# Scatter by accumulation into the residual rows, without four planes, and the last pair of a loop written out

## The chip, the core and the metric

One core of a Trainium2 chip runs the whole program. The metric is the device time of one execution in microseconds. The kernel before took 1590.88 us (median of 3 runs, 1590.01 to 1591.29).

## The reference, cut to what matters

The program is one layer of a diffusion backbone: 512 latent tokens and 256 context tokens of 1024 channels go through a bidirectional gated recurrence (HGRN2) with its projections, and then through a mixture of experts. The change touches only the mixture of experts and the final norm:

```python
def moe(h, router_w, router_b, w1, b1, w2, b2):
    logits = (h @ router_w + router_b).astype(F32)
    top_v, top_i = lax.top_k(logits, TOP_K)          # 4 of 32 experts per token
    top_w = jax.nn.softmax(top_v, axis=-1)
    ...                                              # assignments sorted by expert, cut in blocks
    def block_ffn(args):
        tok, e = args
        z = h[tok] @ w1[e] + b1[e]                   # 1024 -> 2048
        z_glu, z_lin = jnp.split(z, 2, axis=-1)
        z_glu = jnp.minimum(z_glu, SWIGLU_LIMIT)
        z_lin = jnp.clip(z_lin, -SWIGLU_LIMIT, SWIGLU_LIMIT)
        act = z_glu * jax.nn.sigmoid(SWIGLU_ALPHA * z_glu) * (z_lin + 1.0)
        return act @ w2[e] + b2[e]                   # 1024 -> 1024
    ...
    return jnp.zeros_like(h).at[slot_tok].add(y)     # y: rows times their slot weight
```

The layer's output is rmsnorm(r + gate * moe(f)), where r is the residual after the mixer and f its modulated norm. Every token gets four expert outputs, each times its softmax weight, and they are summed. All is float32.

## The kernel before, in words

The first 500 us are the mixer; they are the same in both kernels. Then the routing tables are made, and the expert loop runs. A block is 32 tokens of one expert; a pair is two blocks (par 0 and par 1). Each block is one step. There are as many pairs as the routing needs (`n_pairs`, read by every engine from a small table), so the loop is a hardware loop; the first pair stands in front of it, written out. Weights of an expert are 12 MB (w1 8 MB in eight chunks, w2 4 MB in four) and come from DRAM into one of two places in SBUF (`arena` for par 0, `big_b` for par 1) when a step's expert is a new one. Because 32 tokens fill only a quarter of 128 partitions, every row of 1024 is held as four quarters of 256 in four groups of 32 partitions.

What each engine does in a step (i, par):

- SP (L475 to L503): for each of the eight w1 chunks and four w2 chunks it waits until TensorE has used the old one, and loads the next expert's, or raises the semaphore if the expert stays the same.
- POOL (L642 to L652): `gather` (L619) fetches the token rows of the step two ahead from `frows` in DRAM by an indirect DMA, indexed by `tok_n`; `scatter` (L625) writes the step's result rows `y_sb` to DRAM by an indirect DMA, indexed by `row_s`. Entries without a token have an index out of bounds and are left out.
- TensorE: `rest_of_z` (w1 chunks 6 and 7 of this step, and the bias), `next_z` (w1 chunks 0 to 5 of the next step), `slots_of` (a small product from which the indices of a later step come), and `second` (w2).
- ScalarE: the sigmoid. VectorE: `step` (L1437): the transpose of the next step's gathered rows (`transpose_x`), `moved_rows`, the index of a later step (`index`), the gating (`gated`), the one-hot tiles, and `weighted` (L1431), the step's result times its slot weight and the gate g2.

In the kernel before, the scatter goes to `yrows`, a DRAM tensor of 4 x 512 rows: a plane for each of the four choices k of a token. No two scatters write the same row. The index is token + 512 k; k is carried through the slot product as a further column (`kf`, `kw16[:, :, 0]`), and gives `row_n`. A scatter waits for its rows, and VectorE's `moved_rows` for the scatter of two steps before, because it uses the same index tile. Two empty scatters are issued ahead of the loop.

After the loop SP loads the residual rows `hrows` (512 KB in each of four tiles), b2 four times, and the two broadcast rows g2 and final_g. When both scatter semaphores have reached their count it loads the four planes, 8 MB, as eight pairs of planes (L513 to L517). TensorE puts the residual, the weighted b2 and the planes 2 and 3 into PSUM by products with the identity; VectorE adds planes 0 and 1 and the PSUM banks; ScalarE makes the sum of squares and the root; VectorE scales; SP stores (L518 to L520).

TensorE's loop (L1906) runs over all pairs but the first, and in its last step it also runs `next_z` and `slots_of` for a pair that doesn't exist; the weights' semaphores are raised for it without a load.

Of the kernel before, what the change touches and what calls it, by code (L numbers as in the profile page):

```python
# [5 lines left out]
F32 = mybir.dt.float32  # L6
BF16 = mybir.dt.bfloat16
# [7 lines left out]
P = 128  # L15
# [16 lines left out]
N_CONST = 16  # L32
# [31 lines left out]
def build(nc, x, c, ctx_in, c_ctx, mod_c, mod_w, mod_b, norm1_g, norm2_g, hg_w_in, hg_lb_logits, hg_norm_g,  # L64
          hg_w_out, router_w, router_b, moe_w1, moe_b1, moe_w2, moe_b2, final_g, out):
    frows = nc.dram_tensor("frows", [LAT, D], F32, kind="Internal").ap()
    yrows = nc.dram_tensor("yrows", [TOPK * LAT, D], F32, kind="Internal").ap()
# [3 lines left out]
    yquarters = yrows.rearrange("r (q n) -> (r q) n", q=QT)  # L71
    with ExitStack() as stack:
# [74 lines left out]
        msk16 = sb("msk16", [P, LT, E], BF16)  # L147
# [35 lines left out]
        oh, ohd = (late[:, n * 512:n * 512 + 512].rearrange("p (i k e) -> p i k e", i=LT, k=TOPK) for n in range(2))  # L183
# [27 lines left out]
        kf = sb("kf", [P, LT * TOPK])  # L211
# [3 lines left out]
        row_n = [sb(f"row_n{i}", [P, 1], U32) for i in range(2)]  # L215
# [53 lines left out]
        ygat = arena[:, 0:16384].rearrange("p (i k n) -> p i k n", i=LT, k=TOPK)  # L269
        hx = arena[:, 16384:20480].rearrange("p (i n) -> p i n", i=LT)  # L270
        g2_row, fin_row = arena[:, 20480:21504], arena[:, 21504:22528]
        sq_out, b2_x = arena[:, 22528:23552], arena[:, 23552:24576]
# [26 lines left out]
        w1_used w2_used sel_ok ld_br ring_free h_st mrow_st ld_mrow wdT_ok b2_ok sum_ps fin_sq fin_std fin_ok out_st""".split()  # L299
# [7 lines left out]
        ROWS_IN = 32 + 16 * (LT + QT + 2)  # L307
        gath = [*ld_wh, *ld_mod, *ld_wout]
        GATHERED = [16 * H + 16] * 4 + [16 * DK + 16] * 2 + [32] * 2
# [32 lines left out]
        def _(sp):  # L342
# [161 lines left out]

            for i in range(LT):
                sp.dma_start(hx[:, i, :], hrows[i * P:(i + 1) * P, :]).then_inc(S["ld_rw"], 16)
            for q in range(QT):
                sp.dma_start(b2_x[q * E:(q + 1) * E, :], moe_b2).then_inc(S["ld_rw"], 16)
            sp.dma_start(g2_row, mrows[3].partition_broadcast(P)).then_inc(S["ld_rw"], 16)
            sp.dma_start(fin_row, final_g.partition_broadcast(P)).then_inc(S["ld_rw"], 16)  # L510
            for par in range(2):
                sp.wait_ge(y_st[par], n_pairs * 16 + 16)
            for i in range(LT):  # L513
                for n in range(2):
                    k = 2 - 2 * n
                    sp.dma_start(ygat[:, i, k:k + 2], yrows.rearrange("(k i p) n -> i p k n", k=TOPK, p=P)[i][:, k:k + 2]
                                 ).then_inc(gath[2 * i + n], 16)  # L517
            for i in range(LT):  # L518
                sp.wait_ge(S["fin_ok"], i + 1)
                sp.dma_start(out[i * P:(i + 1) * P, :], ygat[:, i, 0, :]).then_inc(S["out_st"], 16)  # L520
# [4 lines left out]
        def _(pool):  # L525
# [52 lines left out]
            pool.iota(kf[:, :].rearrange("p (i k) -> p i k", i=LT), pattern=[[0, LT], [TOPK * LAT, TOPK]],  # L578
                      base=TOPK * LAT, channel_multiplier=0,
                      allow_small_or_imprecise_dtypes=True).then_inc(S["consts"], 1)  # L580
            for part in range(3):
                pool.wait_ge(S["consts"], 10 + part)
                pool.iota(pmod[part * E:(part + 1) * E, :], pattern=[[0, 1]], base=0, channel_multiplier=1,
                          allow_small_or_imprecise_dtypes=True).then_inc(S["consts"], 1)
            pool.wait_ge(S["consts"], 13)
            pool.iota(kb_row, pattern=[[-1, E]], base=0, channel_multiplier=0,
                      allow_small_or_imprecise_dtypes=True).then_inc(S["consts"], 1)
            pool.wait_ge(S["consts"], 14)
# [24 lines left out]
            for i in range(2):  # L613
                me.mark(pool.memset(xg[i], 0.0))
                me.mark(pool.memset(y_sb[i], 0.0))
                me.mark(pool.memset(row_s[i][:, :], int(FAR)))
# [16 lines left out]
            for par in range(2):  # L633
                scatter(par)
# [7 lines left out]
            def pair(i):  # L642

                for par in range(2):
# [17 lines left out]
        def _(act):  # L662
# [235 lines left out]
            for i in range(LT):  # L898
# [3 lines left out]
                me.mark(A(sq_out, ygat[:, i, 0, :], ACT.Square, accum_out=stat[:, 12 + i:13 + i]))  # L902
# [6 lines left out]
        def _(dve):  # L909
# [330 lines left out]
            me.mark(V.tensor_tensor(ohd[:, :, 0, :], oh[:, :, 2, :], oh[:, :, 3, :], ALU.add))  # L1240
            me.wait()
            me.link(V.tensor_tensor(msk, msk, ohd[:, :, 0, :], ALU.add))
            V.tensor_copy(msk16[:, :, :], msk).then_inc(S["msk_ok"], 1)
# [13 lines left out]
            def index(par, weighted):  # L1257
# [19 lines left out]
            kf4 = kf[:, :].rearrange("p (i k) -> p i k", i=LT)  # L1277
            me.link(V.tensor_tensor(ohd[:, :, :, 0:2], oh[:, :, :, 0:2],
                                    kf4.unsqueeze(3).broadcast_to([P, LT, TOPK, 2]), ALU.mult))
            with nc.allow_low_precision(reason="one nonzero multiple of 2048, exact in bf16"):  # L1280
                me.link(V.tensor_reduce(kw16[:, :, 0, 0:2], ohd[:, :, :, 0:2].rearrange("p i k e -> p i e k"), AX_X, ALU.add))
# [71 lines left out]
            me.mark(V.tensor_scalar(ohd[:, :, 0, :], oh[:, :, 0, :], kf[:, 0:1], None, ALU.mult))  # L1353
            me.wait()
            me.mark(V.tensor_tensor(wd, wd, es.unsqueeze(2).broadcast_to([P, LT, E]), ALU.mult))
            for k in range(1, TOPK):
                to = kw16[:, :, 0, 0:E] if k == TOPK - 1 else ohd[:, :, k, :]
                me.link(V.scalar_tensor_tensor(to, oh[:, :, k, :], kf[:, k:k + 1], ohd[:, :, k - 1, :], ALU.mult, ALU.add))
# [37 lines left out]
            me.mark(V.tensor_scalar(tab_n[:, 0:1], so_far[0:1, E:E + 1], lead[0:1, E:E + 1], 0.5, ALU.add, ALU.mult))  # L1396
# [57 lines left out]
            n_in = 2 * 9 + 1  # L1454
# [10 lines left out]
            def finish(i):  # L1465
                dve.wait_ge(S["fin_std"], i + 1)
                me.link(V.reciprocal(rst[:, 12 + i:13 + i], rst[:, 12 + i:13 + i]))
                V.scalar_tensor_tensor(ygat[:, i, 0, :], ygat[:, i, 0, :], rst[:, 12 + i:13 + i], fin_row,
# [5 lines left out]
            dve.wait_ge(S["ld_rw"], ROWS_IN)  # L1474
            V.tensor_tensor(b2_x, b2_x, g2_row, ALU.mult).then_inc(S["b2_ok"], 1)
            for i in range(LT):
                dve.wait_ge(gath[2 * i + 1], GATHERED[2 * i + 1])
                total = ygat[:, i, 0, :]
# [488 lines left out]
```

## Time and profile before

| what | us |
|---|---|
| median of 3 runs | 1590.88 |
| the profiled execution | 1585.78 |
| its span (first to last instruction) | 1584.0 |
| TensorE busy | 1461.9 |
| VectorE busy | 735.8 |
| ScalarE busy | 261.3 |
| POOL busy | 210.6 |

Of the chain that ended last, 71% is TensorE, 15% DMA, 7% SP's queue and 4% VectorE. TensorE's mean granted clock is 0.961 of full speed. DMA moved 497 MB at a mean of 314 GB/s. Busy time of TensorE is modelled from pipelined matmuls, so it says when the engine had work, not that it worked at its peak. All times of the trace are counted from the start of the span.

### The profile page before, as it was taken

To read this page: it belongs to the slowest core of one execution; us is meant where nothing else is said; L and a number is where in the kernel's file an instruction comes from. 1 tells how busy PE (TensorE), PEld (TensorE's weight loads), DVE (VectorE), ACT (ScalarE), POOL (GpSimd) and SP (SyncE) were. 2 spreads that over 40 slices of the span, in tenths; PEclk is the share of its full clock that TensorE was granted. 3 is DMA by queue.
4 is the path that set the end of the run, shared out by engine and by line. 5 is a ranking of instruction groups with operands and counts; after the bars stand their busy time and mean duration, and the time that the engine had idled before them with its cause. 6 is when DMAs were issued, how large, how long until landed. Compare 5 with 4: busy or idle time off the path is not lost.

```text
span 1584.0 us, 39651 instructions
## 1 busy us (share of the span) xinstructions
PE 1461.9 (92%) x14639; PEld 738.5 (47%) x14639; DVE 735.8 (46%) x2464; ACT 261.3 (16%) x467; POOL 210.6 (13%) x267
## 2 busy tenths in 40 slices
PE   5999999999896899999979999979899979999896
PEld 3658888888653333433323434323333424333232
DVE  4503877777638544443424434424343423434244
ACT  4402555555413200000000000000000000000001
POOL 1000000000051112111211111211121111212110
PEclk9999999999998999999989999979999979999798
DMA  9685211112577999998798999999799998998997
GB/s 388 192 265 148 62 54 53 53 53 57 172 306 274 358 413 407 412 415 347 301 415 339 408 417 417 414 414 417 321 417 416 417 414 321 410 417 344 413 400 295
DMA packets 130857, 497.19 MB, mean 314 GB/s; under 512 B 15356, under 2 KB 48476, under 8 KB 94892
## 3 DMA queue, kind: packets, MB, share of 16 engines
q1 hardware_dynamic: 122396, 479.93, 77.1%
q0 software_dynamic: 8256, 16.81, 2.8%
q8 instruction: 19, 0.31, 0.1%
q14 instruction: 10, 0.08, 0.0%
q10 hardware_dynamic: 176, 0.06, 0.0%
HBM read 484.92 MB, written 17.58 MB: 317 GB/s over the span
## 4 chain that ended last, share of the span: by engine, by line
PE 71%; DMA 15%; SPq 7%; DVE 4%; issue 1%; ACT 1%; ACTq 0%; DVEq 0%; POOLq 0%
PE ps L1838 28%; PE ps L1870 14%; DMA big_b<-in_moe_w 7%; PE ps L1541 6%; PE ps L1542 6%; PE ps L1543 6%; DMA arena<-in_moe_w 5%; SPq L431 4%; PE ps L1720 3%; SPq L425 2%; PE ps L1652 1%; PE ps L1564 1%; DMA arena<-in_final_g 1%; PE ps L1851 1%; PE ps L1666 1%
## 5 line engine op out<-in xcount | busy, mean ns | idle before, releaser
L1838 PE MATMUL ps<-arena,rows 128*32 128x512 f32 x2736 | 318.2, 602 | 26.7 <-DMA arena<-in_moe_w 20.1
L1838 PE MATMUL ps<-big_b,rows 128*32 128x512 f32 x2688 | 316.8, 607 | 21.8 <-DMA big_b<-in_moe_w 21.8
L886 ACT ACTIVATE rows<-ps 128x256 f32<-128x256 f32 x84 | 32.3, 385 | 977.0 <-issue 661.5
L1838 PEld LDWEIGHTS ps<-arena,rows 128*32 128x32 f32 x2736 | 86.8, 111 | 214.0 <-issue 159.2
L1838 PEld LDWEIGHTS ps<-big_b,rows 128*32 128x32 f32 x2688 | 85.5, 111 | 208.1 <-issue 153.3
L1870 PE MATMUL ps<-big_b,rows 128*32 128x256 f32 x2688 | 163.9, 395 | 8.1 <-DMA big_b<-in_moe_w 8.1
L1870 PE MATMUL ps<-arena,rows 128*32 128x256 f32 x2688 | 161.7, 392 | 9.3 <-DMA arena<-in_moe_w 8.5
L1434 DVE SCALAR_TENSOR_TENSOR y_sb<-ps,w_s,g_q 128x256 f32<-128x256 f32 x42 | 20.3, 484 | 261.0 <-PE ps L1870 261.0
L1434 DVE SCALAR_TENSOR_TENSOR rows<-ps,w_s,g_q 128x256 f32<-128x256 f32 x42 | 20.3, 484 | 256.8 <-PE ps L1870 256.8
L1870 PEld LDWEIGHTS ps<-big_b,rows 128*32 128x32 f32 x2688 | 84.2, 113 | 68.1 <-DMA big_b<-in_moe_w 12.9
L1870 PEld LDWEIGHTS ps<-arena,rows 128*32 128x32 f32 x2688 | 84.1, 112 | 67.0 <-DMA arena<-in_moe_w 13.0
L621 POOL DMA_INDIRECT rows<-frows,tok_n x86 | 88.6, 1030 | 113.8 <-issue 61.1
L1541 PE MATMUL ps<-aT_hi,wh_hi 128*128 128x512 f32 x256 | 101.8, 398 | 0.0
L1543 PE MATMUL ps<-aT_hi,wh_lo 128*128 128x512 f32 x256 | 99.8, 390 | 0.0
L1542 PE MATMUL ps<-aT_lo,wh_hi 128*128 128x512 f32 x256 | 99.8, 390 | 0.0
L627 POOL DMA_INDIRECT yrows<-y_sb,row_s x43 | 44.2, 1027 | 386.6 <-issue 386.6
L627 POOL DMA_INDIRECT yrows<-rows,row_s x43 | 44.1, 1026 | 383.9 <-issue 383.0
L1287 DVE TENSOR_SCALAR pt<-slot_io,dm_all 128x128 bf16<-128x128 f32 x340 | 74.3, 281 | 33.0 <-issue 33.0
L561 POOL TENSOR_SCALAR xv_t<-xv_t 96x1024 f32<-96x1024 f32 x1 | 2.8, 2788 | 429.1 <-DMA xv_t<-in_moe_b 429.1
L1543 PEld LDWEIGHTS ps<-aT_hi,wh_lo 128*128 128x128 f32 x256 | 48.0, 188 | 10.4
L1541 PEld LDWEIGHTS ps<-aT_hi,wh_hi 128*128 128x128 f32 x256 | 48.1, 188 | 9.9
L993 DVE TENSOR_TENSOR wh_lo<-ring_t,wh_hi 128x1024 fp32r<-128x1024 f32 x32 | 38.2, 1220 | 30.9 <-ACT wh_hi L733 30.8
(360 smaller groups left out, 1785.0 us busy)
## 6 DMA issues: line engine op xcount, KB each, us to landing
big_b<-in_moe_w SPq DMA_DIRECT2D x204, 1024.0 KB, 14.2
arena<-in_moe_w SPq DMA_DIRECT2D x180, 1024.0 KB, 15.4
ring_t<-in_hg_w_in SPq DMA_DIRECT2D x32, 512.0 KB, 3.9
ogT<-in_mod_w SPq DMA_DIRECT2D x16, 1024.0 KB, 5.0
arena<-yrows SPq DMA_DIRECT2D x8, 1024.0 KB, 12.6
x_sb<-in_x SPq DMA_DIRECT2D x2, 2048.0 KB, 7.9
arena<-in_hg_w_in SPq DMA_DIRECT2D x4, 1024.0 KB, 13.8
arena<-in_mod_c SPq DMA_DIRECT2D x4, 1024.0 KB, 19.7
```

What stands on the lines that cost most here:

```text
L431: sp.dma_start(to, moe_w2[bass.ds(e * FF + 2 * k * P, 2 * P), :].rearrange("(a p) n -> p a n", p=P)).then_inc(ld_w2[par][k], 16)
L621: pool.indirect_dma_start(out=xg[par], out_offset=None, in_=fquarters, in_offset=bass.IndirectOffsetOnAxis(ap=tok_n[par][:, :], axis=0), b ...
L627: pool.indirect_dma_start(out=yquarters, out_offset=bass.IndirectOffsetOnAxis(ap=row_s[par][:, :], axis=0), in_=y_sb[par], in_offset=None, ...
L993: V.tensor_tensor(wh_lo[s][:, :].rearrange("p (k n) -> p k n", k=DK), wh[:, s], wh_hi[s][:, :].bitcast(F32).rearrange("p (k n) -> p k n", ...
L1287: V.tensor_scalar(to[:, i, :], slot_io[:, :], dm_all[:, i, e], None, ALU.is_equal)
L1434: V.scalar_tensor_tensor(y_sb[par], ps[4 + par][:, 0:NW], w_s[par][:, :], g2_q[:, :], ALU.mult, ALU.mult).then_inc(S["y_ok"], 1)
L1541: mm(bank, th, mh, start=start, stop=False)
L1542: mm(bank, th, ml, start=False, stop=False)
L1543: return mm(bank, tl, mh, start=False, stop=stop)
L1720: last = mm(ps[YO_BANK[j]][:, :], ogT[:, k, i * P:(i + 1) * P], wo[n][:, k, :], start=(k == 0), stop=(k == DK - 1))
L1838: last = mm(bank[q * G:(q + 1) * G, :], XT[par][:, pos * G:(pos + 1) * G], w[:, :, q * NW:(q + 1) * NW], start=(pos == 0), stop=False)
L1870: last = mm(y[q * G:(q + 1) * G, 0:NW], aT2[:, (2 * m + a) * G:(2 * m + a + 1) * G], w2_slot(par, m, a)[:, q * NW:(q + 1) * NW], start=(m ...
```

## The change

The scatter goes to the residual rows themselves: `hrows` is seen as quarters, and the indirect DMA adds its rows to what stands there (compute_op=ALU.add). The index is that of the gather, `tok_n`. As two steps can have the same token, a scatter is issued only when the one before it has landed, and the first when the residual rows are stored. k is no longer carried: `kf`, `row_n`, `yrows`, the products with kf on VectorE, the empty scatters and their clears are gone; the first column of `kw16` now holds the mask of chosen experts, which was `msk16`. After the loop SP loads b2 and g2 by halves (`b2_h`, `g2_h`) and final_g, then waits for the scatters, and then loads the four residual tiles; TensorE makes only the weighted b2; VectorE adds PSUM to the residual tile. TensorE's loop ends one pair earlier; the last pair is written out behind it, without `next_z` and `slots_of` of its second step. The count less one is written beside the count by VectorE.

```diff
@@ gpsimd
             def scatter(par):
-                pool.indirect_dma_start(out=yquarters,
+                pool.indirect_dma_start(out=hquarters,
                                         out_offset=bass.IndirectOffsetOnAxis(ap=row_s[par][:, :], axis=0),
-                                        in_=y_sb[par], in_offset=None, bounds_check=TOPK * LAT * QT - 1,
-                                        oob_is_err=False).then_inc(y_st[par], 16)
-            for par in range(2):
-                scatter(par)
+                                        in_=y_sb[par], in_offset=None, bounds_check=LAT * QT - 1,
+                                        oob_is_err=False, compute_op=ALU.add).then_inc(y_st[par], 16)
...
                     pool.wait_ge(S["y_ok"], i * 2 + (par + 3))
+                    if par:
+                        pool.wait_ge(y_st[0], i * 16 + 16)
+                    elif not isinstance(i, int):
+                        pool.wait_ge(y_st[1], i * 16)
                     pool.sem_inc(S["go"], 1)
                     scatter(par)
+            pool.wait_ge(S["h_st"], 16 * LT)
             pair(0)
@@ vector
-                me.mark(V.scalar_tensor_tensor(col(2), got(2), float(-TOPK * LAT), col(0), ALU.add, ALU.add))
-                V.tensor_tensor(tok_n[par][:, :], col(0), col(1), ALU.add)
-                me.wait()
-                V.tensor_tensor(row_n[par][:, :], col(2), col(1), ALU.add).then_inc(S["idx_ok"], 1)
+                V.tensor_tensor(tok_n[par][:, :], col(0), col(1), ALU.add).then_inc(S["idx_ok"], 1)
...
             def moved_rows(i, par):
-                dve.wait_ge(y_st[par], i * 16 + 16)
-                V.tensor_copy(row_s[par][:, :], row_n[par][:, :]).then_inc(S["rows_ok"], 1)
+                if not isinstance(i, int):
+                    dve.wait_ge(y_st[par], i * 16)
+                dve.wait_ge(S["idx_ok"], i * 2 + (par + 1))
+                V.tensor_copy(row_s[par][:, :], tok_n[par][:, :]).then_inc(S["rows_ok"], 1)
...
-            me.mark(V.tensor_scalar(tab_n[:, 0:1], so_far[0:1, E:E + 1], lead[0:1, E:E + 1], 0.5, ALU.add, ALU.mult))
+            me.link(V.tensor_scalar(tab_nn[:, 0:1], so_far[0:1, E:E + 1], lead[0:1, E:E + 1], 0.5, ALU.add, ALU.mult))
+            me.mark(V.tensor_copy(tab_n[:, 0:1], tab_nn[:, 0:1]))
+            me.mark(V.tensor_scalar(tab_n[:, 1:2], tab_nn[:, 0:1], 1.0, None, ALU.subtract))
...
+            dve.wait_ge(S["ld_b2"], 32 * QT)
+            V.tensor_tensor(b2_h, b2_h, g2_h, ALU.mult).then_inc(S["b2_ok"], 1)
+            dve.wait_ge(S["sum_ps"], 2)
+            dve.wait_ge(S["ld_fin"], 16)
             for i in range(LT):
-                me.link(V.tensor_tensor(total, total, ygat[:, i, 1, :], ALU.add))
+                dve.wait_ge(ld_hx[i], HX_IN)
                 for n in range(2):
-                    V.tensor_tensor(total[:, c0], total[:, c0], ps[2 * i + n][:, :], ALU.add).then_inc(S["fin_sq"], 1)
+                    V.tensor_tensor(hx[:, i, c0], hx[:, i, c0], ps[2 * i + n][:, :], ALU.add).then_inc(S["fin_sq"], 1)
@@ sync
+            for q in range(QT):
+                c0 = (q % 2) * 512
+                sp.dma_start(b2_h[q * E:(q + 1) * E, :], moe_b2[:, c0:c0 + 512]).then_inc(S["ld_b2"], 16)
+                sp.dma_start(g2_h[q * E:(q + 1) * E, :], mrows[3, c0:c0 + 512].partition_broadcast(E)).then_inc(S["ld_b2"], 16)
+            sp.dma_start(fin_row, final_g.partition_broadcast(P)).then_inc(S["ld_fin"], 16)
+            for par in range(2):
+                sp.wait_ge(y_st[par], n_pairs * 16)
             for i in range(LT):
+                sp.dma_start(hx[:, i, :], hrows[i * P:(i + 1) * P, :]).then_inc(ld_hx[i], 16)
@@ tensor
-            with pe.Fori(1, n_pairs) as i:
+            with pe.Fori(1, last_pair) as i:
                 for par in range(2):
                     step(i, par)
+            step(last_pair, 0)
+            rest_of_z(last_pair, 1)
+            second(last_pair, 1)
...
             for b in range(2 * LT):
                 r = slice((b % QT) * E, (b % QT) * E + E)
+                last = mm(ps[b][:, :], wdT[r, (b // 2) * P:(b // 2 + 1) * P], b2_h[r, :], start=True, stop=True)
+            last.then_inc(S["sum_ps"], 1)
```

## Rows read from the trace of the kernel before

**Rows 1.** Chain that ended last, in order of time: start us, us, what

```profile
706.82 22.80 DMA big_b<-in_moe_w
```

**Rows 2.** Windows of the loop: stretch, us, busy (x) by engine, PEclk, DMA share, GB/s

```profile
535.00:730.00 195.00, 188.24 (x2364) 74.95 (x2359) 82.34 (x371) 6.54 (x17) 35.85 (x35) 1.00 1.00 407
776.00:843.00 67.00, 56.57 (x656) 20.53 (x652) 22.59 (x102) 1.93 (x5) 9.88 (x10) 0.92 0.96 389
848.00:1136.00 288.00, 269.19 (x3208) 101.21 (x3200) 111.00 (x502) 8.86 (x23) 47.16 (x46) 0.95 1.00 409
1147.00:1302.00 155.00, 141.68 (x1644) 52.14 (x1640) 57.23 (x258) 4.62 (x12) 24.61 (x24) 0.92 1.02 416
1342.00:1422.00 80.00, 76.31 (x953) 30.08 (x952) 33.49 (x151) 2.69 (x7) 14.37 (x14) 1.00 1.01 414
1448.00:1541.00 93.00, 85.18 (x988) 31.65 (x980) 33.27 (x150) 2.69 (x7) 14.36 (x14) 0.91 1.02 415
```

**Rows 3.** Timeline of a steady step: start us, us, engine, line, tiles [idle before]

```profile
1347.64 1.02 POOL L627 DMA_INDIRECT yrows<-y_sb,row_s  x1 [8.11 <-issue]
...
1349.45 1.03 POOL L621 DMA_INDIRECT rows<-frows,tok_n  x1 [0.79 <-issue]
...
1357.55 0.44 DVE L1248 STREAM_TRANSPOSE rows<-rows 128x256 f32<-128x256 f32 x1
...
1358.50 1.02 POOL L627 DMA_INDIRECT yrows<-rows,row_s  x1 [8.03 <-issue]
...
1358.83 5.33 PE L1838 MATMUL ps<-arena,rows 128*32 128x512 f32 x48
```

**Rows 4.** The DMA view: queue q0 (packets, MB, share), indirect DMAs (count, median us to landing)

```profile
q0 software_dynamic: 8256, 16.81, 2.8%
...
rows<-frows,tok_n POOLq DMA_INDIRECT x86, 6.1
...
yrows<-rows,row_s POOLq DMA_INDIRECT x43, 5.9
```

**Rows 5.** Line L627, the scatters

```profile
DMA to landing us min/median/max: 2.3/5.9/6.8
```

**Rows 6.** Timeline, start of the loop

```profile
511.53 1.05 POOL L621 DMA_INDIRECT rows<-frows,tok_n  x1 [25.27 <-DVE row_n L1269]
```

**Rows 7.** Timeline, end of the loop

```profile
1534.17 0.45 DVE L1421 STREAM_TRANSPOSE rows<-rows 128x256 f32<-128x256 f32 x1
...
1537.61 3.66 PE L1870 MATMUL ps<-big_b,rows 128*32 128x256 f32 x64
1541.34 0.48 DVE L1434 SCALAR_TENSOR_TENSOR y_sb<-ps,w_s,g_q 128x256 f32<-128x256 f32 x1 [5.26 <-PE ps L1870]
...
1542.69 1.35 POOL L627 DMA_INDIRECT yrows<-y_sb,row_s  x1 [8.10 <-issue]
...
1550.78 6.78 SPq L516 DMA_DIRECT2D arena<-yrows  x8
```

**Rows 8.** Line L431, the last w2 chunk

```profile
L431 SPq DMA_DIRECT2D big_b<-in_moe_w x1: 822/822/822, 1519.7 to 1519.7; - x1
...
DMA to landing us min/median/max: 19.3/19.3/19.3
```

**Rows 9.** Line L516, the loads of the planes

```profile
L516 SPq DMA_DIRECT2D arena<-yrows x8: 377/514/2420, 1550.8 to 1555.1; - x8
...
DMA to landing us min/median/max: 4.8/12.6/19.6
```

**Rows 10.** Timeline of the tail

```profile
1567.99 1.28 ACT L904 ACT_TABLE_LOAD   x1
...
1576.63 1.28 DVE L1483 TENSOR_TENSOR arena<-arena,ps 128x512 f32<-128x512 f32 x2
...
1577.95 1.06 ACT L902 ACTIVATE arena<-arena 128x1024 f32<-128x1024 f32 x1 [2.37 <-DVE arena L1483]
...
1579.65 1.28 DVE L1468 SCALAR_TENSOR_TENSOR arena<-arena,rst 128x1024 f32<-128x1024 f32 x1
```

More of the change, by code:

```diff
@@ L31 @@
 EPS = 1e-6
-N_CONST = 16
+N_CONST = 15
 LIMIT = 7.0
@@ L182, in build @@
         i8f = rtake(LT * 8).rearrange("p (i e) -> p i e", i=LT)
-        oh, ohd = (late[:, n * 512:n * 512 + 512].rearrange("p (i k e) -> p i k e", i=LT, k=TOPK) for n in range(2))
+        oh, oh_sum = (late[:, n * 512:n * 512 + 512].rearrange("p (i k e) -> p i k e", i=LT, k=TOPK) for n in range(2))
         msk = rtake(LT * E).rearrange("p (i e) -> p i e", i=LT)
@@ L268, in build @@
         y_sb = [mv(7), nc.alloc_sbuf_tensor_at("y_sb1", [P, NW], F32, offset=place["res"])[:, :]]
[L269 to L272, printed above, removed]
+        hx = arena[:, 0:4096].rearrange("p (i n) -> p i n", i=LT)
+        fin_row, sq_out = arena[:, 4096:5120], arena[:, 5120:6144]
+        b2_h, g2_h = arena[:, 6144:6656], arena[:, 6656:7168]
         wd4 = ogT[:, 0, :].rearrange("p (i q e) -> p i q e", i=LT, q=QT)
@@ L503, in _ @@
                     over_w1(AHEAD, W1C)
-            for i in range(LT):
[L506 to L510, printed above, removed]
-            for par in range(2):
[L512 to L517, printed above, removed]
+            for q in range(QT):
[5 more added lines that the diff above has]
+                sp.wait_ge(y_st[par], n_pairs * 16)
+            for i in range(LT):
+                sp.dma_start(hx[:, i, :], hrows[i * P:(i + 1) * P, :]).then_inc(ld_hx[i], 16)
             for i in range(LT):
                 sp.wait_ge(S["fin_ok"], i + 1)
-                sp.dma_start(out[i * P:(i + 1) * P, :], ygat[:, i, 0, :]).then_inc(S["out_st"], 16)
+                sp.dma_start(out[i * P:(i + 1) * P, :], hx[:, i, :]).then_inc(S["out_st"], 16)
             sp.wait_ge(S["out_st"], 16 * LT)
@@ L1275, in choose @@
                                 pmod[0:96, :], None, ALU.is_equal).then_inc(S["sel_ok"], 1)
[L1277 to L1281, printed above, removed]
             ranks = ps[0][:, 0:LT * E].rearrange("p (i e) -> p i e", i=LT)
@@ L1352, in _ @@
             me.mark(V.reciprocal(es, es))
-            me.mark(V.tensor_scalar(ohd[:, :, 0, :], oh[:, :, 0, :], kf[:, 0:1], None, ALU.mult))
             me.wait()
             me.mark(V.tensor_tensor(wd, wd, es.unsqueeze(2).broadcast_to([P, LT, E]), ALU.mult))
-            for k in range(1, TOPK):
-                to = kw16[:, :, 0, 0:E] if k == TOPK - 1 else ohd[:, :, k, :]
-                me.link(V.scalar_tensor_tensor(to, oh[:, :, k, :], kf[:, k:k + 1], ohd[:, :, k - 1, :], ALU.mult, ALU.add))
+            me.wait()
             dve.sem_inc(S["late_free"], 1)
@@ L1809, in _ @@
             for i in range(LT):
-                last = mm(ps[6][0:E, 0:2], msk16[:, i, :], ones16[:, 0:2], start=(i == 0), stop=(i == LT - 1))
+                last = mm(ps[6][0:E, 0:2], kw16[:, i, 0, 0:E], ones16[:, 0:2], start=(i == 0), stop=(i == LT - 1))
             last.then_inc(S["tab_ps"], 1)
@@ L1901, in _ @@
             pe.wait_ge(S["tab_ok"], 1)
-            n_pairs = pe.value_load(tab_n[0:1, 0:1], min_val=2, max_val=NPAIR_MAX)
+            last_pair = pe.value_load(tab_n[0:1, 1:2], min_val=1, max_val=NPAIR_MAX - 1)
             second(0, 0)
@@ L1905, in _ @@
             step(0, 1)
-            with pe.Fori(1, n_pairs) as i:
+            with pe.Fori(1, last_pair) as i:
                 for par in range(2):
                     step(i, par)
-            pe.wait_ge(S["y_ok"], n_pairs * 2 + 2)
-            for q in range(QT):
-                mm(ps[2][q * G:(q + 1) * G, :], sel[0][:, :], b_z[:, :, q * NW:(q + 1) * NW], start=False, stop=True)
+            step(last_pair, 0)
+            rest_of_z(last_pair, 1)
+            second(last_pair, 1)
+            pe.wait_ge(S["y_ok"], last_pair * 2 + 4)
             pe.wait_ge(S["b2_ok"], 1)
```

58 lines of the change are left out of this document (14 added, 44 removed).

## The prediction

> **What bounds the kernel now.** I read the chain of waits first [rows 1], then the windows by stage, then single steps in the timeline. In the expert loop (about 535 to 1541 us) two things are nearly full at once: TensorE, and the 16 DMA engines that fetch each expert's 12 MB of weights. A step that waits for nothing takes 10.86 us: one scatter starts at 1347.64, the next at 1358.50 [rows 3]. Which of the two sets the end has to be asked per stretch. Weight loads stand in SP's queue in order, so as long as the DMA engines stay full, the landing that TensorE stalls on is late by everything they carried since they were last idle. The windows show six such stretches, each at 407 to 416 GB/s (389 in the short one, which holds an idle end), each beginning where the engines had run idle and ending at TensorE's last stall before the next idle [rows 2]; the chain's own DMA pieces, such as the 22.80 us at 706.82, sit at their ends [rows 1]. Together they are 195 + 67 + 288 + 155 + 80 + 93 = 878 us of the loop's 1006. Between them TensorE sets the pace. So in seven eighths of the loop a byte more on the DMA engines is paid for, and a TensorE instruction is not.
>
> After the loop nothing overlaps: the last `second` (1537.61 + 3.66), the last scatter (starts 1542.69), its landing (SP goes on at 1550.78), 8 MB of planes back, four tiles of sums and norms, the store [rows 7 to 10].
>
> **The last pair outside the loop.** TensorE no longer computes the six idle chunks behind the last `rest_of_z`. Their cover was not useless: `second` needs aT2, whose transpose ends at 1534.17 + 0.45 = 1534.6, so it could start 2.9 us earlier [rows 7]. But what is late next is a weight load. The last of its four w2 chunks is issued at 1519.7 and lands 19.3 us later, at 1539.0 [rows 8]. Behind it a quarter of `second` is left (16 matmuls, about 1.1 us): end 1540.1 in place of 1541.3. Gain 1.2 us, not 2.9.
>
> **The last landing.** From the end of `second` to the scatter's start: 1542.69 less 1541.27 = 1.4 us, unchanged, so it starts at 1541.5. Landing took 8.1 us (1542.69 to 1550.78) behind 3.5 MB that SP had queued: the residual rows, b2 and two broadcast rows. Now 1.0 MB is queued there (b2_h and g2_h 256 KB each, fin_row 512 KB). Scatters in the loop land in 2.3 to 6.8 us [rows 5]. An accumulate has a read of its destination to make first. Bounds 3 and 8; I take 5, between the empty queue's 2.3 and the full queue's 5.9, as the queue is short but the read is added: 1546.5.
>
> **The tail.** Old: from 1550.8 to 1584.0, 33.2 us. New: only the four residual tiles are loaded, 512 KB each. The eight plane pairs of 1 MB were issued from 1550.78 to 1555.1; the first landed 4.8 us after its issue, the last 19.6 after its own, at 1574.7, so they came some 2.7 us apart [rows 9]. Half a megabyte then takes 1.35 us, and the first one 4.8 - 1.35 = 3.45. First tile at 1550.2 (with 0.2 for SP), the fourth at 1554. VectorE then does per tile two adds (1.28), reciprocal and gap (0.2), the scaling (1.28): 2.8 us. The first add of the old tail (L1479) is gone, and so is TensorE's part in the tail. ScalarE's part between adds and scaling takes 1.7 us (it starts at 1577.95, the scaling at 1579.65), plus 1.28 once for the table [rows 10]. Played through: adds of tile 0 end 1551.5, its square root (with the table) 1554.3, its scaling 1555.8; tile 2's adds 1557.1, tile 1 scaled 1558.6, tile 3's adds 1559.9, tile 2 scaled 1561.4; tile 3's square root 1561.5, scaled 1563.0. Store as before, 1580.93 to 1584.0 = 3.1 us: end 1566.1. TensorE's b2 product is hidden: b2_h lands near 1541.5, and product and eight matmuls are over by 1546.5 even at half clock, before the first tile is there; without that cover it would cost at most 2 to 4 us. Landing and tail together: 1584.0 - 1566.1 = **17.9 us gained**, the 1.2 us of TensorE included; 15 to 20 with the landing's bounds.
>
> **Start of the loop.** The index is ready one operation earlier on VectorE (about 0.2 us), and the first gather at 511.53 hangs on it [rows 6]: gain 0.2 us. The one-hot products with kf (four instructions near 518 to 520), the clears and the two empty scatters lay beside the gather's flight: nothing. The three small instructions for last_pair run while VectorE waits for TensorE's table: nothing, at most 0.3 us lost.
>
> **The loop.** Per step VectorE drops two small instructions, far from its 10.86 us. POOL gets a wait: scatter n is not issued until scatter n-1 has landed. Queued behind the waiting scatter is the next gather, for which VectorE's transpose waits, and for that TensorE's `next_z`. Scatter to scatter is 10.86 us; from a satisfied wait to the start of the next scatter is 0.9 us (1541.82 to 1542.69), so the wait is free while a scatter lands within 10.0 us. Plain ones need 5.9, at most 6.8 [rows 5]. The gather (1349.45, 6.1 us) is in at 1355.6, its transpose begins at 1357.55 and TensorE needs it at 1358.83 [rows 3, 4]: 2.0 us of slack, 2.8 with what the transpose leaves.
>
> What is not free is the DMA work. No row shows an accumulate. A scatter's rows must now be read in DRAM as well as written: between nothing (the read runs where the engines have room) and two passes more over the same bytes (read and write each once more, or small packets that stream badly). The nearest row is the gather, which is a read of just these bytes: queue q0 carries gathers and scatters alike, 16.81 MB, so 8.4 MB each [rows 4]. One pass more of 8.4 MB at 415 GB/s is 20.2 us over 84 filled scatters (86 less the two empty ones), 0.24 us each. The six stretches hold 35 + 10 + 46 + 24 + 14 + 14 = 143 indirect transfers [rows 2], half of them scatters: 71 x 0.24 = **17.0 us lost**. I take one pass; bounds 0 and 34.
>
> The Trainium skill ("Collectives: The Full Stack", section on the bandwidth ceiling) says an add in the DMA engines costs no time by itself but needs two source reads in the same ring, and so runs at half a copy's rate. By that rule too the scatters would cost one pass more; no trace here can show it yet. The Trainium skill ("DMA: Bandwidth & Descriptors", latency table) gives 2 us for an HBM access at high load; by an estimate from it an accumulate would land after 5.9 + 2 = 7.9 us, short of the 10.0 at which the new wait decides.
>
> **Sum.** 1584.0 - 17.9 - 0.2 + 17.0 = 1582.9 us of span. The profiled execution took 1585.78 us, 1.8 more than its span; the median of the three runs is 5.1 us above it. I carry over the difference: 1590.88 - 1.1 = **1589.8 us**. No change is what a measurement of this kernel can't tell apart: within 0.2%, 3.2 us.
>
> **The rivals.**
> - *The read is hidden* (under 0.6 of a pass). For: a load keeps an engine's read and its write going at once, and if the write is the narrower of the two there is room to read. Against: the busy share stands at 1.02, and nothing in it shows room. The loop loses 0 to 10 us, the tail gain stays: 1573 to 1583, middle 1579.
> - *The accumulate is dearer than a pass* (slower). Place: the DMA engines in the six stretches. With p passes more, the loop loses 17.0 p against 18.1 gained; it decides from p = 1.06, that is from 0.26 us of all 16 engines per scatter. At p = 2: 1590.9 - 18.1 + 34 = 1607. For: rows are small pieces of 1 KB and each needs two inputs. Against: plain scatters and gathers lose nothing by their size now.
> - *One by one becomes the pace.* Over 10.0 us of landing, each step costs the excess, and the next gather slips with it. At 12 us: 84 x 2 = 168 us, less some 70 us of stalls on weights that it would fill, less the tail: about 1670. For: every landing is now in series. Against: more than 3 us of room over the slowest plain landing.
> - *The tail does not shrink as said*, because the last landing or the b2 product is late by 8 us or more: 1598.
>
> **Chances.** One pass, 0.6 to 1.4 of it (1583 to 1597): 0.38. Hidden: 0.27. Dearer: 0.21. Pace: 0.10. Tail: 0.04. Below 0.88 of a pass the time is under 1587.7, above 1.25 over 1594.1, so the forecast's own case splits into faster 0.14, same 0.16, slower 0.08; of the dearer case 0.02 lies within the 0.2% still. Faster 0.27 + 0.14 = 0.41, same 0.16 + 0.02 = 0.18, slower 0.08 + 0.19 + 0.10 + 0.04 = 0.41. Range: leaving out the pace case, the dearest part of the dearer one and the tail's upper bound: 1573 to 1612; the likeliest case alone 1583 to 1597.
>
> **What would show it.** The tail: SP's loads of hx from about 1546 plus the loop's shift, and from there to the end 19 to 20 us in place of 33. `second` of the last step still waiting for a w2 chunk. The loop: steady steps still 10.86 us; more stall of TensorE on moe_w; queue q0's share of the engines up from 2.8% to some 4%; the span between the first weight load behind an idle and the last stall longer by 0.24 us per scatter. A POOL wait in front of scatters that ends on a landing, and steady steps over 10.9 us, would mean the pace rival. I am wrong if q0's share stays at 2.8% (then it is faster by over 10 us) or reaches 6%.

## The result and the profile after

Changed kernel: 1594.72 us (median of 20 runs, 1586.13 to 1599.89). Kernel before, beside it: 1590.48 us (20 runs). The ratio is 1.0029, 95% interval 1.0017 to 1.0041: 0.29% slower, some 4.6 us. Forecast was 1589.8, 1.1 us faster. The profiled execution took 1596.19 us, its span is 1594.4.

In the changed kernel the scatter is L612, the gather L606, the matmuls of `next_z`/`rest_of_z` L1817, `second` L1849, the loads of the residual tiles L507.

The queues of the page (packets, MB, share of the 16 engines), against [rows 4]:

```profile
q1 hardware_dynamic: 120268, 471.01, 74.7%
q0 software_dynamic: 16224, 16.82, 5.0%
```

The add shows as twice the packets and a share of 5.0% for 2.8%; the megabytes stay, since the page books the rows once and not the read at their destination. The packets are cut differently too: in the packet records a plain scatter puts four rows of 1 KB into a packet of 4096 B (2004 such packets before), an adding one sends each row as a packet of its own (8192 of 1024 B). The instruction list of L612, against [rows 5]:

```profile
L612 POOL DMA_INDIRECT hrows<-rows,row_s x42: 1587/1589/1637, 543.3 to 1557.3; - x42
...
DMA to landing us min/median/max: 3.8/8.1/9.6
```

An adding scatter lands in 8.1 us in place of 5.9, at most 9.6, and takes GpSimd 1.59 us in place of 1.02. The timeline of steady steps, POOL alone (start, us, idle before):

```profile
600.66 1.59 POOL L612 DMA_INDIRECT hrows<-y_sb,row_s  x1 [7.91 <-DVE row_s L1350]
602.57 1.05 POOL L606 DMA_INDIRECT rows<-frows,tok_n  x1 [0.31 <-issue]
611.54 1.59 POOL L612 DMA_INDIRECT hrows<-rows,row_s  x1 [7.93 <-DVE row_s L1350]
```

Scatter to scatter is 10.88 us: as before [rows 3], so the new wait for the scatter before isn't the pace. GpSimd waits for VectorE's index, not for a landing.

Windows (length, busy time and count by engine, granted clock, DMA share, GB/s): one that holds two pauses of the DMA engines, one in which they are full, and the loop from the third gather to the last; first after, then before:

```profile
735.00:870.00 135.00, 124.36 (x1476) 46.54 (x1472) 52.05 (x215) 4.23 (x11) 29.07 (x22) 0.95 0.86 331
870.00:1110.00 240.00, 223.23 (x2672) 83.95 (x2668) 90.55 (x371) 7.31 (x19) 50.18 (x38) 0.95 1.03 408
539.34:1559.21 1019.87, 946.70 (x11224) 354.96 (x11216) 392.41 (x1617) 31.91 (x83) 219.17 (x166) 0.95 0.98 385
```

```profile
735.00:870.00 135.00, 124.57 (x1504) 47.76 (x1500) 52.67 (x238) 4.24 (x11) 22.57 (x22) 0.96 0.88 358
870.00:1110.00 240.00, 226.07 (x2712) 85.65 (x2704) 94.75 (x428) 7.70 (x20) 40.50 (x40) 0.96 1.02 414
535.60:1533.55 997.95, 937.01 (x11236) 356.91 (x11232) 395.07 (x1782) 31.96 (x83) 170.17 (x167) 0.96 0.97 394
```

Where the engines were full they are still full and the page books 1.4% less a second (408 for 414). Queue q0 carries 3.86 MB from 870 to 1110 us, half of it scatters; with their 1.9 MB read once more at the destination, 8 GB/s, it would be 416 (an estimate: no record shows that read). Where the engines pause, their share did not rise. TensorE's waits on weights went up with it. The two longest groups of PE's waits in the loop, from 540 us on (total us, times, longest), after and before:

```profile
PE ps L1817 <- DMA big_b<-in_moe_w: 29.1, 26, 2.0
PE ps L1817 <- DMA arena<-in_moe_w: 22.9, 18, 2.4
```

```profile
PE ps L1838 <- DMA big_b<-in_moe_w: 21.8, 21, 1.9
PE ps L1838 <- DMA arena<-in_moe_w: 20.1, 15, 2.3
```

From the third gather to the last the loop takes 1019.9 us against 997.9. By the two windows above, TensorE is idle for 12.2 us more of it and busy for 9.7 us more. Its clock goes with the waits: by the clock records it stands at the lower of its two levels (1.2 GHz) for 105.8 us of this stretch, and for 81.9 before.

The end of the kernel after, in the timeline, against [rows 7, 10]:

```profile
1564.71 1.07 PE L1849 MATMUL ps<-big_b,rows 128*32 128x256 f32 x16 [2.73 <-DMA big_b<-in_moe_w]
1568.27 1.94 PE L1849 MATMUL ps<-big_b,rows 128*32 128x256 f32 x16 [2.48 <-DMA big_b<-in_moe_w]
1570.27 0.48 DVE L1414 SCALAR_TENSOR_TENSOR y_sb<-ps,w_s,g_q 128x256 f32<-128x256 f32 x1 [8.75 <-PE ps L1849]
1571.77 1.77 POOL L612 DMA_INDIRECT hrows<-y_sb,row_s  x1 [11.51 <-issue]
1575.64 1.77 SPq L507 DMA_DIRECT2D arena<-hrows  x4
1578.96 2.48 DVE L1462 TENSOR_TENSOR arena<-arena,ps 128x512 f32<-128x512 f32 x4 [6.28 <-DMA arena<-hrows]
1590.08 1.28 DVE L1448 SCALAR_TENSOR_TENSOR arena<-arena,rst 128x1024 f32<-128x1024 f32 x1
```

`second` waits for the last pieces of w2; the last scatter is in after 3.9 us (1571.77 to 1575.64); from there to the end are 18.8 us, where it was 33.2. From the last w2 piece to the end of the span: 1594.4 - 1568.3 = 26.1 us, before 1584.0 - 1539.0 = 45.0 [rows 8]. So the profile shows 18.9 us won behind the last w2 piece and 22.0 lost in the loop. Two smaller parts complete the 10.4 us between the spans: 3.7 us ahead of the third gather, and 3.6 us between the last gather and the last w2 piece (9.1 for 5.5). The profiled execution before is 4.7 us under its median and the one after 1.5 above, so the medians are only 4.2 us apart; against the run without the add (999.3 us in the same stretch of the loop) the loop loses 20.5.

### The profile page after: what moved, and what is told of

Read it like the earlier page. It is cut to its first block, busy times and chain, and to the rows that moved or that the text cites. A ratio compares the mean times of both kernels' runs of the same rounds, so it can differ in the third digit from the quotient of the medians.

```text
span 1594.4 us, 39326 instructions
## 1 busy us (share of the span) xinstructions
PE 1453.9 (91%) x14535; PEld 730.0 (46%) x14535; DVE 728.7 (46%) x2284; ACT 261.1 (16%) x467; POOL 257.7 (16%) x260
## 4 chain that ended last, share of the span: by engine, by line
PE 65%; DMA 17%; SPq 9%; DVE 5%; issue 2%; ACT 1%; ACTq 0%; DVEq 0%; POOLq 0%
PE ps L1817 24%; PE ps L1849 13%; DMA big_b<-in_moe_w 9%; DMA arena<-in_moe_w 7%; PE ps L1520 6%; PE ps L1521 6%; PE ps L1522 6%; SPq L425 5%; SPq L419 3%; PE ps L1699 2%; PE ps L1543 1%; PE ps L1631 1%; PE ps L1645 1%; PE ps L1640 1%; DMA rows<-frows,tok_n 1%
## 5 line engine op out<-in xcount | busy, mean ns | idle before, releaser
L1817 PE MATMUL ps<-big_b,rows 128*32 128x512 f32 x2688 | 321.7, 613 | 29.2 <-DMA big_b<-in_moe_w 29.1
L1817 PE MATMUL ps<-arena,rows 128*32 128x512 f32 x2688 | 316.7, 608 | 29.7 <-DMA arena<-in_moe_w 22.9
L1817 PEld LDWEIGHTS ps<-big_b,rows 128*32 128x32 f32 x2688 | 84.3, 111 | 221.8 <-issue 151.1
L1817 PEld LDWEIGHTS ps<-arena,rows 128*32 128x32 f32 x2688 | 85.3, 111 | 216.8 <-issue 155.3
L1849 PE MATMUL ps<-big_b,rows 128*32 128x256 f32 x2688 | 165.6, 397 | 16.4 <-DMA big_b<-in_moe_w 13.9
L1849 PE MATMUL ps<-arena,rows 128*32 128x256 f32 x2688 | 163.0, 393 | 9.0 <-DMA arena<-in_moe_w 8.1
L612 POOL DMA_INDIRECT hrows<-rows,row_s x42 | 66.9, 1592 | 393.1 <-DVE row_s L1350 382.2
L612 POOL DMA_INDIRECT hrows<-y_sb,row_s x42 | 66.9, 1594 | 389.8 <-DVE row_s L1350 362.4
L1849 PEld LDWEIGHTS ps<-big_b,rows 128*32 128x32 f32 x2688 | 84.2, 113 | 78.3 <-DMA big_b<-in_moe_w 20.2
L1849 PEld LDWEIGHTS ps<-arena,rows 128*32 128x32 f32 x2688 | 84.1, 113 | 68.2 <-DMA arena<-in_moe_w 13.5
L606 POOL DMA_INDIRECT rows<-frows,tok_n x86 | 90.5, 1052 | 79.9 <-DVE tok_n L1253 54.0
## 6 DMA issues: line engine op xcount, KB each, us to landing
arena<-in_mod_c SPq DMA_DIRECT2D x4, 1024.0 KB, 18.8
```

What stands on the lines that cost most here:

```text
L606: pool.indirect_dma_start(out=xg[par], out_offset=None, in_=fquarters, in_offset=bass.IndirectOffsetOnAxis(ap=tok_n[par][:, :], axis=0), b ...
L612: pool.indirect_dma_start(out=hquarters, out_offset=bass.IndirectOffsetOnAxis(ap=row_s[par][:, :], axis=0), in_=y_sb[par], in_offset=None, ...
L1817: last = mm(bank[q * G:(q + 1) * G, :], XT[par][:, pos * G:(pos + 1) * G], w[:, :, q * NW:(q + 1) * NW], start=(pos == 0), stop=False)
L1849: last = mm(y[q * G:(q + 1) * G, 0:NW], aT2[:, (2 * m + a) * G:(2 * m + a + 1) * G], w2_slot(par, m, a)[:, q * NW:(q + 1) * NW], start=(m ...
```

## The experiments

My theory: the add costs what its extra bytes cost on full DMA engines, about one more pass of the rows, and the new tail pays what the timeline says. Rivals: the order among the scatters, the longer instruction or descriptor work is the price; the price is that of small packets and not of bytes; the last pair's new place has a part in it. All ratios are to the kernel before, run on the same chip beside them.

**The changed kernel without the add.** The rows overwrite the residual rows, so the sum is left out.

```diff
-   oob_is_err=False, compute_op=ALU.add).then_inc(y_st[par], 16)
+   oob_is_err=False).then_inc(y_st[par], 16)
```

> The changed kernel with a plain scatter in place of the adding one (same order, same waits; the sum over the four experts and the residual is left out). Theory A, the add's own DMA work sets the loop: queue q0's share goes back from 5.0% to 2.8% and the loop loses some 25 to 30 us, so about 1568 us, 22 us under the kernel before. Theory B, the one-by-one order (its wait and the later gathers) costs the loop: the time stays near 1592.

Measured: 1572.59 us, ratio 0.9899 (0.9879 to 0.9920). Its line of q0, and its scatters:

```profile
q0 software_dynamic: 8160, 16.81, 2.9%
```

```profile
DMA to landing us min/median/max: 2.5/5.8/6.7
```

Everything in the change but the add is worth 1.0% or 16.1 us of gain. The add alone takes 1.0029 - 0.9899 = 1.3%, 20.7 us; by the two intervals it is 17 to 24.5. More was expected: 25 to 30 us, about 1568. All waits between scatters are still there in this kernel, so the order is not the price.

**The planes kept, the new tail alone.** Scatters as before, into four planes and in no order; tail and last pair from the change. The planes are not read back, so the expert outputs are left out.

```diff
- out=hquarters, ... bounds_check=LAT * QT - 1, oob_is_err=False, compute_op=ALU.add)
+ out=yquarters, ... bounds_check=TOPK * LAT * QT - 1, oob_is_err=False)
- pool.wait_ge(y_st[0], i * 16 + 16)     # scatter n waits for scatter n-1
```

> The kernel before with the new tail and the last pair outside TensorE's loop; its scatters go unordered into the four planes as before, which are not read (the expert sum is left out). Both theories: the tail alone gives 18 to 19 us, so about 1572. Against e1_no_add this prices the order by itself: theory A says the two agree within 3 us, theory B says that this one is some 20 us faster than e1_no_add.

Measured: 1575.02 us, 0.9902 (0.9883 to 0.9920), the same as with ordered plain scatters, to within some 4 us by the intervals. One by one costs nothing that shows here, and neither does the smaller target.

**The kernel before with a second scatter** of the same rows into spare planes: 8.4 MB more, plain and unordered.

```diff
+ for rows in (yquarters, zquarters):
      pool.indirect_dma_start(out=rows, ..., in_=y_sb[par], ...)
```

> The kernel before with every scatter issued twice, the second into spare planes that nothing reads: 8.4 MB of plain writes more. Theory A, the loop pays for DMA bytes in the stretches where the engines are full (seven eighths of it): 20.2 us of engine time times 0.83 = 17 us slower, about 1607. Rival, TensorE sets the loop and the engines have room (as the chain of waits alone suggests, 65% TensorE against 17% DMA): under 5 us, 1590 to 1595.

Measured: 1612.86 us, 1.0136 (1.0113 to 1.0158): 21.6 us, by the interval 18 to 25. Its queue:

```profile
q0 software_dynamic: 12384, 25.22, 4.1%
```

This prices the unit in which the forecast reckoned. One plain pass more costs 21.6 us, where the sum would have charged it 17.0; the add costs the same as this pass, as nearly as it can be told. The clock goes the same way: 102.4 us of the loop at the lower level, for 81.9 before (85.3 in the changed kernel without the add).

**The kernel before with the last pair outside the loop.**

```diff
- with pe.Fori(1, n_pairs) as i:
+ with pe.Fori(1, last_pair) as i:
      ...
+ step(last_pair, 0); rest_of_z(last_pair, 1); second(last_pair, 1)
- mm(ps[2][q * G:(q + 1) * G, :], sel[0][:, :], b_z[...])   # idle chunks
```

> The kernel before with only the last pair put outside TensorE's loop. By the landing of the last w2 chunk, which sets the end of the last product: 1.2 us gained or less, about 1589.5; in the trace the last step's L1870 product starts some 3 us earlier and then waits for its weights. If the cover of the idle chunks were all of it: 2.9 us.

Measured: 1590.02 us, 0.9996 (0.9978 to 1.0014). The 1.2 us forecast is inside the interval, and so is nothing at all. The timeline shows the expected wait in its place, though:

```profile
1549.10 1.07 PE L1872 MATMUL ps<-big_b,rows 128*32 128x256 f32 x16 [1.54 <-DMA big_b<-in_moe_w]
1550.24 0.48 DVE L1436 SCALAR_TENSOR_TENSOR y_sb<-ps,w_s,g_q 128x256 f32<-128x256 f32 x1 [5.36 <-PE ps L1872]
```

`second` ends on its last w2 piece and VectorE follows 1.1 us behind it, as the prediction had it.

**Nearly all rows dropped, plain and adding.** All instructions, waits and index lists stay; a bound of 0 lets row 0 alone through. The expert outputs' way to DRAM is left out. The first is the run with the planes kept, the second the changed kernel.

```diff
- bounds_check=TOPK * LAT * QT - 1      (adding: LAT * QT - 1)
+ bounds_check=0
```

> The run that scatters into the four planes with the changed kernel's tail (1575.0 us), with nearly every scattered row dropped by its bound: all scatters are still issued, in the same order and with the same waits, but only row 0 moves. It leaves out the expert outputs' way to DRAM. My theory, that a scatter costs the loop the time its bytes take from full DMA engines and nothing else: one plain pass of 8.4 MB in and 8.4 MB out goes, which measured 21.6 us where it was added a second time, so 1553 to 1556 us. Rival, that only some stretches of the loop pay and the rest is cover: 1562 us or more. Second rival, that the descriptors' making and the waits are the cost: 1572 us or more.

> The changed kernel, with nearly every row of the adding scatter dropped in the same way: the add's descriptors, its instruction on GpSimd and its waits stay, its bytes go. It leaves out the expert outputs' way to DRAM. My theory, that the add costs its destination traffic alone: equal to the plain scatter with rows dropped, within 4 us (1552 to 1558 us), and so 37 to 43 us under the changed kernel. Rival, that the order among the scatters or the longer instruction on GpSimd carries part of the 20.7 us: it stays 8 to 20 us above the plain one with rows dropped.

Measured: plain 1563.80 us, 0.9825 (0.9793 to 0.9857); adding 1562.54 us, 0.9821 (0.9788 to 0.9853). First point: they are equal, so of the add's 20.7 us nothing is left once its rows don't move. That equality was expected (the fall under the changed kernel, 33 us, is less than the 37 to 43 I gave), and it speaks against the rival: the instruction is as long as before. The adding scatter without its rows still lands in 7.4 us, and the plain one in 5.7, so most of its longer landing isn't the rows' either. The landings, plain and adding:

```profile
DMA to landing us min/median/max: 2.1/5.7/6.7
DMA to landing us min/median/max: 2.7/7.4/9.0
```

The page of the adding one, its queue and the line:

```profile
q0 software_dynamic: 16224, 8.50, 1.9%
...
L612 POOL DMA_INDIRECT hrows<-rows,row_s x42 | 67.0, 1595 | 373.9 <-DVE row_s L1350 370.9
```

Second point, a miss: I expected 20 us from dropping the plain pass and got 0.9902 - 0.9825 = 0.8%, 12 us (6 to 18 by the intervals). From the third gather to the last the loop goes from 1000.9 to 989.6 us. With 1563.8 us it falls where the rival put it (only some stretches pay, the rest is cover: 1562 or more). But had part of the pass lain in the pauses, they would have grown without it. The idle time of the DMA engines over the six pauses of the loop, summed from the records, was 50 us with the pass and is 48 without. The windows of the plain one show another reason: what is left streams more slowly.

```profile
870.00:1110.00 240.00, 228.03 (x2764) 88.12 (x2764) 95.34 (x430) 7.70 (x20) 40.97 (x40) 0.96 1.02 410
1170.00:1290.00 120.00, 108.36 (x1304) 41.05 (x1296) 43.02 (x194) 3.47 (x9) 18.45 (x18) 0.95 1.02 413
```

Of the same stretches with the pass, in the run with the planes kept:

```profile
870.00:1110.00 240.00, 225.74 (x2712) 85.69 (x2708) 95.38 (x430) 7.67 (x20) 40.95 (x40) 0.96 1.02 415
1170.00:1290.00 120.00, 109.29 (x1288) 40.36 (x1280) 44.13 (x201) 3.45 (x9) 18.43 (x18) 0.94 1.02 416
```

**Expert rows in bf16.** The kernel before with the last pair outside, and rows of 512 B in place of 1 KB; the tail reads 4.2 MB of planes back for 8.4 and TensorE adds all four with a bf16 identity. As in the changed kernel, b2 and g2 come by halves and VectorE adds the residual rows, so the tail's part isn't that of the bytes alone. Each expert's output row is rounded to bf16.

```diff
- yrows = nc.dram_tensor("yrows", [TOPK * LAT, D], F32, ...)
+ yrows = nc.dram_tensor("yrows", [TOPK * LAT, D], BF16, ...)
- for k in (2, 3): mm(ps[2 * i + n], ident, ygat[:, i, k, ...])
+ for k in range(TOPK): mm(ps[2 * i + n], id16, ygat[:, i, k, ...])
```

> The kernel before with the last pair outside TensorE's loop, and with the experts' output rows in bf16: the scatter writes rows of 512 B into four planes, the tail reads 4.2 MB of planes back in place of 8.4 MB and TensorE sums all four with a bf16 identity; the residual rows are added by VectorE. It rounds each expert's output row to bf16. My theory, that bytes in a full loop are the price: the loop gives back half a pass, 10 to 11 us, and the tail half of its readback, some 10 us, so 1567 to 1572 us, below both kernels. Rival, that a row's cost is its packet and not its bytes: the loop gives back nothing and the tail 5 to 10 us, so 1580 to 1585 us.

Measured: 1570.95 us, 0.9872 (0.9843 to 0.9901): 1.3% below before and 1.6% below the changed kernel, the fastest version that still carries the expert outputs. The total is where it was expected, its parts are not. The loop (third gather to last) gave 999.5 - 994.8 = 4.7 us and not 10.8; from the last scatter's issue to the end of the span it went from 43.2 to 28.8 us, 14.4 and not 10. The half pass taken away is worth less than half of the pass put on, as with the dropped rows. It is no test of small packets: by the packet records the plain scatter puts eight of the 512 B rows into one packet of 4096 B. Its queue, and in the timeline the four loads of the planes and TensorE's sums behind the first of them:

```profile
q0 software_dynamic: 6880, 12.62, 2.2%
```

```profile
1548.41 2.11 SPq L517 DMA_DIRECT2D arena<-yrows  x4
1553.36 9.99 PE L1928 MATMUL ps<-arena,ogT 128*128 128x512 bf16 x32 [4.20 <-DMA arena<-yrows]
```

**Scatters by themselves.** Groups of eight scatters of 128 rows, nothing beside them; the whole computation is left out.

```diff
+ for w, dt, add in cases:      # w in 256, 512, 1024; f32, bf16; plain, adding
+     for k in range(8): pool.indirect_dma_start(out=rows, ..., in_=z[:, 0:w], ...)
+     ... wait for all, then four clears of 1 us as a pause
```

> Indirect scatters alone, with no weights beside them: eight scatters of 128 rows each, one after the other, for rows of 256, 512 and 1024 numbers in f32 and in bf16, plain and adding, each set apart by a pause. The whole computation is left out. My theory (a fixed part for a packet plus its bytes, and about double the time at the destination when it adds): at 1 KB rows the adding packets take 1.5 to 2.5 times the plain ones, and at 4 KB rows the ratio is lower, 1.0 to 1.5. Rival (the add costs by bytes): the same ratio at all row lengths. Packets of 512 B against 1 KB: more than half the time by the fixed part, half of it by bytes alone.

The windows of eight of its groups (length, POOL busy, clock, DMA share, GB/s), in pairs of plain and adding: f32 rows of 2 KB, of 4 KB, then bf16 rows of 512 B and of 1 KB.

```profile
108.60:120.20 11.60, 7.86 (x8) 1.00 0.48 182
125.20:143.80 18.60, 12.44 (x8) 1.00 0.84 113
148.90:162.40 13.50, 7.79 (x8) 1.00 0.79 311
167.40:191.80 24.40, 12.43 (x8) 1.00 0.92 172
196.90:208.00 11.10, 7.85 (x8) 1.00 0.14 47
213.00:229.00 16.00, 12.42 (x8) 1.00 0.35 33
234.10:245.40 11.30, 7.85 (x8) 1.00 0.26 93
250.40:266.90 16.50, 12.39 (x8) 1.00 0.54 64
```

Share times length times 16 engines over 1024 rows is one engine's time for a row. At 1 KB: plain 0.26 x 11.3 x 16 / 1024 = 46 ns, adding 139 ns, ratio 3.0. At 512 B 24 and 88 ns (3.6), at 2 KB 87 and 244 (2.8), at 4 KB 167 and 351 (2.1). The groups of f32 rows of 1 KB, the kernel's own, agree with the bf16 ones: 47 and 138 ns by q0's share alone. The ratio falls with the row as expected, but all of it lies higher than I said (1.5 to 2.5 at 1 KB, 1.0 to 1.5 at 4 KB).

The two kinds of scatter differ in their packets as well. q0 at rows of 1 KB, plain and adding, and at rows of 4 KB, plain and adding:

```profile
q0 software_dynamic: 384, 1.05, 26.0%
q0 software_dynamic: 1152, 1.05, 53.8%
...
q0 software_dynamic: 1152, 4.19, 78.9%
q0 software_dynamic: 1152, 4.19, 91.5%
```

In each group 128 packets of 4 B go beside the rows. The other 256 of the plain 1 KB group carry four rows each, and the adding group has 1024, one for each row. So plain rows go nearly by bytes, some 41 ns per KB, because they share packets of 4096 B. Only at 4 KB is the packet the same in both, and there the add takes 2.1 times, one more pass. What lies above that at shorter rows comes with the small packets. No run sends plain rows one to a packet, so their share is not shown.

## Why the prediction was wrong

**What failed: the size of the loop's term.** The prediction put "71 x 0.24 = 17.0 us lost", one pass at 415 GB/s charged in the six stretches alone. The add measured 20.7 us and the plain second pass 21.6. All 84 scatters at 0.24 are 20.2. The 13 that I took as free lie outside the stretches, 128 us of the loop in which I took the DMA engines to have room. In more than half of that time they were as full as inside: a stretch ended at TensorE's last stall, but the engines streamed on until their pause. Three windows of the kernel before, 74 us:

```profile
735.00:767.00 32.00, 32.00 (x408) 12.89 (x404) 13.77 (x64) 1.16 (x3) 5.64 (x6) 1.00 1.00 408
1302.00:1330.00 28.00, 28.00 (x344) 10.80 (x340) 14.14 (x64) 1.16 (x3) 6.15 (x6) 1.00 1.02 415
1422.00:1436.00 14.00, 14.00 (x160) 4.92 (x156) 4.77 (x21) 0.39 (x1) 2.05 (x2) 0.88 1.02 411
```

And a byte put there or in the pauses wasn't free either. The engines' idle time, summed from the records over the six pauses between 725 and 1480 us, stayed: 46 us before, 49 after, 49 without the add, 50 with the second scatter. An extra pass did not go into the pauses; it moved them. The loss also has a part that the forecast had no term for: with the waits the clock fell (105.8 us at the lower level for 81.9, and 71.7 and 68.3 with the rows dropped). In a full stretch a slower product mostly takes from the wait for the next weights; that is argued, and no run separates it. How much of the 3.7 us missed is which and how much is the interval of the add (17 to 24.5) can't be settled by these runs.

**Why that was enough for a wrong sign.** The sum was a difference of two terms of nearly one size: -17.9 - 0.2 + 17.0. The rest of the miss is smaller: tail, last pair and start together measured -16.1 (12.7 to 19.2 of gain) against -18.1. Here too one step was wrong. The forecast let the last w2 chunk land 19.3 us after its issue, as before; in the changed kernel it takes 23.1:

```profile
L425 SPq DMA_DIRECT2D big_b<-in_moe_w x1: 1124/1124/1124, 1545.1 to 1545.1; - x1
...
DMA to landing us min/median/max: 23.1/23.1/23.1
```

It is 22.0 to 23.1 us in five kernels in which the small loads of b2, g2 and final_g stand next in SP's queue, and 19.3 to 20.5 in the three that load the residual tiles there. While it is in flight the engines bring 293 GB/s from 1559 to 1565 us at a share of 1.09; before, 403 GB/s from 1533 to 1539 us at 1.03. So the last `second` ends 11.0 us behind the last gather, for 7.7 before, where 1.2 us less was forecast; from the w2 chunk on the new tail wins 18.9, 1.0 more than the sum had.

The rival "accumulate dearer than a pass" named p = 1.06, in its unit of 17.0 us, as the point of the sign's change; the runs give 20.7 / 17.0 = 1.2 (1.0 to 1.4 by the interval). So it decided, but not by its mechanism: against the second plain scatter the add is at 0.96 of a pass.

**What held.**
- The tail: 18.8 us from the residual tiles' loads to the end (19 to 20 forecast); the last landing 3.9 us (5 taken, bounds 3 and 8); 18.9 us won from the last w2 piece on, in the profile.
- `second` waiting for w2 in the end, in both kernels shown. By itself its gain of 1.2 us is too small for these runs to show.
- The pace: steps stay at 10.88 us and landings under the 10.0 us, with 0.4 us left over the longest. The estimate from the Trainium skill ("DMA: Bandwidth & Descriptors", "Latency and other measured facts") was 7.9 us, with 2 us for an HBM access at high load; the trace has 8.1. The nearness is luck: with its rows dropped the adding scatter still takes 7.4, and the plain one 5.7.
- Hidden reading is out. The case for it was that no more than 0.6 of a pass would show; 1.0 did.
- The start of 0.2 us is lost in what comes before it: the first gather is at 509.5 to 518.3 us in the profiles of this case.

**The indicator that misled.** I wrote that q0's share of about 4% would fit and 6% would not; it is 5.0%. By the records' time the add costs more than a pass: q0's packets add up to 80.0 us of all 16 engines, against 44.8 before. That is 35.2 us, and the loop lost 22.0. The adding packets of 1 KB take 101 ns each (median; mean 108), and plain ones 40 ns per KB (160 for 4 KB). A share of 1.03 means that packet records overlap, so part of that time was not taken from others; which part is not shown. Share tells that a resource is in use; what a use costs is told by the span.

The Trainium skill ("Collectives: The Full Stack", section on the bandwidth ceiling) has the adding DMA read two sources and run at half a copy's rate. In the loop the price fits it, one pass more, and so do the scatters alone at rows of 4 KB, where both kinds have the same packets (2.1). At 1 KB rows they do not: 139 ns against 46 is a third of the rate, with one row in a packet against four.

**What the change is, in the end.** It took 8.4 MB of reading out of the tail, where nothing covered it, and put the add, with 8.4 MB of reading at the scatters' destination, into a loop whose DMA engines have nothing to spare: 16.1 us won, 20.7 lost. The runs show that the 20.7 us come with the rows that the add moves, and not with order, instruction or waits. That it is their reading and not their smaller packets is the likelier by the plain second pass and by the rate above, but it is not shown. The bf16 planes take bytes away on both sides and win on both.

## What to carry to other kernels

An adding scatter is not a free sum: here each row cost the loop what one more plain copy of it would have cost. It should pay if the readback it saves is exposed and the DMA engines beside the scatter have room (no run here had such room); if they are full, cut the bytes (row type, fewer planes) before moving them. Where a forecast is the difference of two large terms, price the unit of each by a run that doubles it, and don't credit pauses of the bound engine as cover until something is seen to go into them.

## What was not expected of the hardware

- The last pass taken away is worth less than the next one put on: -12 us (6 to 18) for dropping the scatters' bytes, +21.6 (18 to 25) for doubling them. With the bytes gone the weights stream at 410 GB/s over 870 to 1110 us, where the kernel before moves 414 ([rows 2] have 409 over a wider stretch). 1% of 1000 us is 10 us, about what is missing. Why weights and gathers stream at the lower rate without the scatters' rows is open.
- An adding scatter takes GpSimd 1.59 us, against 1.02 for a plain one, whether its rows are dropped or not.
- An adding scatter sends every row as a packet of its own, a plain one fills packets of 4096 B with rows of 512 B to 2 KB. Engine time of a row: adding 88, 139, 244 and 351 ns at 512 B, 1, 2 and 4 KB, plain 24, 46, 87 and 167.
- Where the small loads of b2, g2 and final_g stand right behind it in SP's queue, the last w2 chunk lands after 22.0 to 23.1 us in place of 19.3 to 20.5.
